# Gated linear attention's result: 16 TensorE transposes replaced by VectorE block transposes and SBUF transfers

## The reference, cut to what matters

```
o_gla = gated_linear_attention(...)                      # [256 tokens, 4 heads x 256]
o_gla = rms_norm_2(o_gla, gla_out_norm_g).reshape(b, s, 1024) * silu(p_r)
gates = sigmoid(p_gate + branch_gate_bias).reshape(b, s, 2, 1024)
mixed = gates[:, :, 0] * (o_attn @ w_attn_branch) + gates[:, :, 1] * (o_gla @ w_gla_branch)
x = x + mixed @ w_out
```

## Time and profile before

| | |
|---|---|
| median of 3 runs | 791.87 us |
| span of the profiled execution, first to last instruction | 790.3 us |
| median of the runs above that span | 1.57 us |
| PE busy | 785.6 us (99%), 4684 matmuls |
| DVE busy | 594.2 us (75%) |
| ACT busy | 469.6 us (59%) |
| DMA traffic | 143.49 MB, mean 182 GB/s |

### The profile page before, as it was taken

One profiled execution on the slowest core, in us unless ns is written; L12 is line 12 of the kernel. 1 busy time (PEld: TensorE's weight loads), 2 busy tenths in 40 slices (PEclk: granted clock), 3 DMA queues, 4 the chain that ended last, 5 costly groups with the idle time before them and its releaser, 6 DMA issues.

```text
span 790.3 us, 12177 instructions
## 1 busy us (share of the span) xinstructions
PE 785.6 (99%) x4684; PEld 667.0 (84%) x4684; DVE 594.2 (75%) x977; ACT 469.6 (59%) x673; POOL 4.5 (1%) x16
## 2 busy tenths in 40 slices
PE   9999999999999999999999999999999999999998
PEld 7888889888888888888888888888888888888886
DVE  6996789987878788679898973677775765556654
ACT  6876556655656666987566655656644654434542
POOL 0000000000000000000000000010000000000000
PEclk9999999999999999999999999999999999999999
DMA  9873354664655663736645376323656555665551
GB/s 325 285 256 107 108 160 160 214 208 164 203 187 194 200 229 113 248 125 212 211 140 182 107 243 230 107 82 134 216 174 194 171 189 177 211 201 177 181 185 53
DMA packets 84653, 143.49 MB, mean 182 GB/s; under 512 B 3904, under 2 KB 44672, under 8 KB 84352
## 3 DMA queue, kind: packets, MB, share of 16 engines
q1 hardware_dynamic: 83888, 141.82, 54.4%
q10 hardware_dynamic: 720, 1.05, 0.4%
HBM read 141.29 MB, written 1.05 MB: 180 GB/s over the span
## 4 chain that ended last, share of the span: by engine, by line
PE 98%; DMA 1%; ACTq 0%; ACT 0%; DVE 0%; issue 0%
PE bank L539 21%; PE bank L540 21%; PE bank L541 21%; PE bank L628 15%; PE bank L633 8%; PE bank L401 3%; PE bank L1039 2%; PE bank L1041 1%; PE bank L612 1%; PE bank L1106 1%; PE bank L1179 1%; DMA arena<-in_x_turned 1%; PE bank L1208 1%; PE bank L615 0%; PE bank L786 0%; PE bank L1136 0%
## 5 line engine op out<-in xcount | busy, mean ns | idle before, releaser
L1901 DVE TENSOR_TENSOR w_lo<-raw,w_hi 128x1024 fp32r<-128x1024 f32 (+1 forms) x254 | 302.5, 1215 | 55.0 <-ACT w_hi L1350 54.2
L1350 ACT CAST w_hi<-raw 128x1024 fp32r<-128x1024 f32 (+1 forms) x254 | 259.8, 1047 | 122.9 <-PE bank L541 112.9
L539 PE MATMUL bank<-w_hi,h_both 128*128 128x512 f32 x352 | 140.4, 399 | 0.0
L540 PE MATMUL bank<-w_lo,h_both 128*128 128x512 f32 x352 | 137.5, 391 | 0.0
L541 PE MATMUL bank<-w_hi,h_both 128*128 128x512 f32 x352 | 137.4, 390 | 0.0
L539 PE MATMUL bank<-w_hi,a_both 128*128 128x512 f32 (+1 forms) x318 | 124.6, 392 | 0.0
L540 PE MATMUL bank<-w_lo,a_both 128*128 128x512 f32 (+1 forms) x318 | 123.6, 389 | 0.0
L541 PE MATMUL bank<-w_hi,a_both 128*128 128x512 f32 (+1 forms) x318 | 123.6, 389 | 0.0
L628 PE MATMUL bank<-a_both,w_hi 128*128 128x512 f32 x512 | 121.5, 390 | 0.0
L628 PEld LDWEIGHTS bank<-a_both,w_hi 128*128 128x128 f32 x512 | 95.5, 188 | 19.3
L539 PEld LDWEIGHTS bank<-w_hi,h_both 128*128 128x128 f32 x352 | 66.2, 188 | 14.4 <-issue 1.5
(11 more groups left out here) (242 smaller groups left out, 891.6 us busy)
## 6 DMA issues: line engine op xcount, KB each, us to landing
raw<-in_w_in SPq DMA_DIRECT2D x45, 1024.0 KB, 5.2
raw<-in_w_up SPq DMA_DIRECT2D x22, 1024.0 KB, 5.1
raw<-in_w_ff_up SPq DMA_DIRECT2D x16, 1024.0 KB, 5.4
raw<-in_w_ff_down SPq DMA_DIRECT2D x16, 1024.0 KB, 5.0
raw<-in_w_down SPq DMA_DIRECT2D x11, 1024.0 KB, 4.9
raw<-in_w_out SPq DMA_DIRECT2D x8, 1024.0 KB, 5.1
raw<-in_w_gla_branch SPq DMA_DIRECT2D x4, 1024.0 KB, 5.1
raw<-in_w_attn_branch SPq DMA_DIRECT2D x2, 1024.0 KB, 5.1
```

The lines of the kernel that those rows point to most:

```text
L539: nc.tensor.matmul(dst, l_hi, r_hi, start=start, stop=False)
L540: nc.tensor.matmul(dst, l_hi, r_lo, start=False, stop=False)
L1350: nc.scalar.copy(dst, raw_half(m % RAW, half, size, cols)).then_inc(s.hi_done, 1)
L1901: nc.vector.tensor_tensor(dst, raw_half(n // 2 % RAW, n % 2, size, cols), h, ALU.subtract).then_inc(s.lo_done, 1)
```

## The change

GLA's result is no longer turned by PE. For each token tile a, DVE turns every 32 x 32 block of the 128 x 1024 tile in place of its partition group (`turn_go`, one instruction into `go_blocks`). SP then issues 16 transfers from SBUF to SBUF (`move_go`), each of 32 partitions x 256 numbers (1 KB of each partition, 32 KB in all), which carry block row i, block column j to block row j, block column i. ACT multiplies the tile by the gain and puts the blocks in order (two instructions of 128 x 512, each waited for), then rounds (one of 128 x 1024) (`go_hi`). DVE makes the low part (`go_lo`). `go_scaled` runs two loop steps earlier in part, so that a tile is complete when its turn comes. Two pairs of semaphores are merged or dropped.

```
-            for m in range(M_GATE + 1, M_FF2):
+            def move_go(a, moves):
+                for n in moves:
+                    i, j = n // 4, n % 4
+                    sp.dma_start(goT[32 * j:32 * j + 32, a, i], go_blocks[32 * i:32 * i + 32, a, j]).then_inc((s.go_in0, s.go_in1)[a], 16)
+            for m in range(M_GATE + 1, M_GATE + 8):
+                load(m)
+            sp.wait_ge(s.go_blocked, 1)
+            move_go(0, range(6))
+            load(M_GATE + 8)
+            move_go(0, range(6, 12))
+            load(M_GATE + 9)
+            move_go(0, range(12, 16))
+            sp.wait_ge(s.go_blocked, 2)
+            move_go(1, range(16))
+            for m in range(M_GATE + 10, M_FF2):
                 load(m)
...
-            pe.wait_ge(s.gla_ready, 1)
-            pe.wait_ge(s.att_masked, 2 * AH)
-            pe.wait_ge(s.gate_free, 6)
-            turn_tiles(4, lambda a, k: go[:, a, k * P:(k + 1) * P], s.go_turned, (0, 1))
-            fill(2)
-            pe.wait_ge(s.att_pt, AH)
-            turn_tiles(4, lambda a, k: go[:, a, 512 + k * P:640 + k * P], s.go_turned, (4, 5))
+            fill(4)
             att_value(AH - 2)
             att_value(AH - 1)
-            fill(4)
+            fill(2)
+            pe.wait_ge(s.att_masked, 2 * AH)
...
-            pe.wait_ge(s.go_lo, 4)
+            pe.wait_ge(s.go_lo, 2)
...
+            def go_hi(a):
+                act.wait_ge((s.go_in0, s.go_in1)[a], 256)
+                for half in range(2):
+                    tiles = goT[:, a].rearrange("p i (k h t) -> p h k i t", h=2, t=32)[:, half]
+                    dst = go_gained[:, a].rearrange("p (k h) (i t) -> p h k i t", h=2, i=4)[:, half]
+                    link(nc.scalar.activation(dst, tiles, ACT.Copy, scale=column("gla_out_norm_g_2", half)))
+                nc.scalar.copy(h2_hi[:, :, a * P:(a + 1) * P], go_gained[:, a]).then_inc(s.go_hi, 1)
...
-            turned_hi(a_hi, 4, 4, s.go_turned, 0, lambda k: column("gla_out_norm_g_2", k % 2), s.go_hi, (0, 1))
-            turned_hi(a_hi, 8, 4, s.go_turned, 2, lambda k: column("gla_out_norm_g_2", k % 2), s.go_hi)
+                if v == AH - 1:
+                    go_hi(0)
+            go_hi(1)
...
+            def turn_go(a):
+                dve.wait_ge(s.gla_ready, a + 1)
+                nc.vector.transpose(go_blocks[:, a].rearrange("p j (k t) -> p k j t", t=32),
+                                    go[:, a].rearrange("p (k j c) -> p k j c", j=4, c=32)).then_inc(s.go_blocked, 1)
+            def go_lo(a):
+                dve.wait_ge(s.go_hi, a + 1)
+                ts = slice(a * P, (a + 1) * P)
+                nc.vector.tensor_tensor(h2_lo[:, :, ts], go_gained[:, a], h2_hi[:, :, ts].bitcast(F32), ALU.subtract).then_inc(
+                    s.go_lo, 1)
...
-            turned_lo(a_lo, a_hi, 4, 4, s.go_hi, 0, lambda k: column("gla_out_norm_g_2", k % 2), s.go_lo, (0, 1))
-            turned_lo(a_lo, a_hi, 8, 4, s.go_hi, 2, lambda k: column("gla_out_norm_g_2", k % 2), s.go_lo)
+            go_lo(0)
+            go_lo(1)
             gate_scaled(3)
```

More of the change, by code:

```diff
@@ L196 @@
 SEMAPHORES = (
-    "x_in first_x0 first_x1 first_x2 first_x3 first_x4 first_w0 first_w1 first_w2 first_w3 first_w4 first_w5 first_w6 first_x_top first_x_lo first_x_hi first_w_hi first_w_lo slab2_half act_warm pe_warm ident_in pos_in consts_in decay_in vecs_in fw_in gate_up_in levels_in dil_in v_far_in out_stored "
+    "x_in first_x0 first_x1 first_x2 first_x3 first_x4 first_w0 first_w1 first_w2 first_w3 first_w4 first_w5 first_w6 first_x_top first_x_lo first_x_hi first_w_hi first_w_lo slab2_half warmed ident_in pos_in consts_in decay_in vecs_in fw_in gate_up_in levels_in dil_in v_far_in out_stored "
     "hi_done lo_done mm_done acc_free0 acc_free1 "
@@ L216 @@
     "gla_e gla_qe gla_level gla_taken gla_o gla_go gla_ssq gla_ready gate_free gate_done "
-    "go_turned go_hi go_lo "
+    "go_blocked go_in0 go_in1 go_hi go_lo "
     "att_squared att_ms root_guessed root_found att_scaled att_turned att_T "
     "att_scores att_masked att_exp att_normed att_turnedp att_pt att_pv oa_hi oa_lo "
-    "bias_in gate_half mix_scaled mix_taken mix_ready mix_turned mix_hi mix_lo "
+    "bias_in gate_half mix_scaled mix_ready mix_turned mix_hi mix_lo "
     "up_low up_summed up_square up_hi up_lo last_down"
@@ L370, in two_blocks_kernel @@
         go_squares = area(7168, GH * GV)
+        go_blocks = area(0, TT, 4, 8 * 32)
+        goT = area(5120, TT, 4, 8 * 32)
+        go_gained = area(0, TT, 8, P)
         gates = (area(3072, TT, D), area(7168, TT, D))
@@ L663, in h_ready @@
                 return lambda k: pe.wait_ge(s.h_lo_done, 4 * norm + k // 2 + 1) if k % 2 == 0 else None
-            pe.wait_ge(s.pe_warm, 1)
+            pe.wait_ge(s.warmed, 1)
             for _ in range(4):
@@ L1394, in _ @@
                 load_x(q)
-            act.wait_ge(s.act_warm, 1)
+            act.wait_ge(s.warmed, 2)
             nc.scalar.copy(st[:, 95:96], st[:, 94:95])
@@ L1953, in rotate @@
                 return nc.vector.tensor_tensor(x2, x2, t1, ALU.add)
-            nc.vector.memset(warm, 0.0).then_inc(s.pe_warm, 1)
-            nc.vector.memset(st[:, 94:95], 0.0).then_inc(s.act_warm, 1)
+            nc.vector.memset(warm, 0.0).then_inc(s.warmed, 1)
+            nc.vector.memset(st[:, 94:95], 0.0).then_inc(s.warmed, 1)
             for k in range(KT):
@@ L2497, in go_scaled @@
                                                          silu_r[:, r, cols], ALU.mult, ALU.mult)
-                if pair_ == GH - 1:
+                if pair_ % 2 == 1:
                     ins.then_inc(s.gla_ready, 1)
+            def turn_go(a):
[7 more added lines that the diff above has]
+                    s.go_lo, 1)
             dve.wait_ge(s.dil_in, 16)
@@ L2520, in _ @@
                         dve.wait_ge(acc_free[c % 2], c // 2 + 1)
-                if 3 <= v < 7:
-                    go_scaled(v - 3)
+                if v == 3:
+                    go_scaled(0)
+                    go_scaled(1)
+                elif v == 4:
+                    turn_go(0)
+                    go_scaled(2)
+                elif v == 5:
+                    go_scaled(3)
                 if v == 5:
@@ L2528, in _ @@
                     out_lo(0)
+                if v == 5:
+                    turn_go(1)
                 if v == 0:
@@ L2581, in _ @@
             dve.wait_ge(s.acc_free1, 14)
-            mixed(1, slice(0, 1)).then_inc(s.mix_taken, 1)
+            mixed(1, slice(0, 1))
             dve.wait_ge(s.mm_done, n + 12)
```

## The result

The changed kernel takes 799.92 us (median of 5 runs, 798.96 to 800.42) against 792.03 us of the kernel before in 5 runs: a ratio of 1.0096, 95% interval 1.0086 to 1.0107. It is slower by 7.9 us. Slower was forecast, by 1.9 us to 793.8 us, and 799.92 lies outside the range of 791.3 to 796.9 us.

A forecast was written before the change was run, and what follows sets the result against it. PE's queue was taken to bound the kernel: PE saves 1.8 us of transposes, then waits 3.7 us for `go_lo`, so the span of 790.3 us becomes 792.2; with 1.57 us outside it, 793.8 us. Range 791.3 to 796.9 us.

The forecast's parts named there:

- PE's saving: On PE, GLA's 16 transposes fall away ahead of GLA's product: 1.78 us.
- The transpose: DVE's turning of one 128 x 1024 tile: 1.2 us, upper bound 2.2 us.
- its covers: On DVE, idle time and waits hide the earlier `go_scaled` and tile 0's transpose; PE's `lo` has 1.6 us to spare.
- SP's load: Load of M_BR + 1 on SP, ahead of 20 moves, issued at 538.5 us after DVE's `lo`.
- Landing of the last move: Tile 1's last move lands 2.0 us after its issue at 548.8 us, at 550.8 us.
- What lies outside the span: Measured time of a run above the profile's span: 1.57 us, as in the kernel before.
- The rival of slow forms: DVE transposes of 2.2 us each give 795.8 us, scattered instructions on ACT 795.0 us; chance 0.12.
- the cheap issue: SP's moves follow each other in less than 0.39 us, so ACT sets the end: 791.3 us; chance 0.22.
- the whole gain: The chain to `go_lo` is done by 550.73 us, PE saves its 1.8 us: 790.1 us; chance 0.03.
- One sum: Upper end of the forecast's case, SP's moves at 0.45 to 0.58 us: 792.5 to 795.2 us; chance 0.53.
- I take 0.52 us: SP's step from one move's issue to the next, bounds 0.41 and 0.57 us; last move issued at 548.8 us.
- The second term that was missing: Clock falls in PE's wait; first half of GLA's product at half speed loses 2.7 us more: 796.5 us; chance 0.10.

The follow-up runs named there:

- e3: Changed kernel with tile 1's moves carrying 8 numbers of each partition instead of 256, all moves still issued: 799.33 us.
- e8: Kernel before with 28 unused transfers behind SP's last load, in four groups of seven, from HBM or SBUF, 32 or 128 partitions: 791.84 us.
- e2: Changed kernel with 27 unneeded matmuls on PE ahead of its wait for the turned result: 797.46 us.
- e4: Changed kernel with all remaining moves of tile 0 and those of tile 1 ahead of the second load of the GLA weights: 795.93 us.
- e6: Changed kernel with moves ahead of that load, five of tile 1 issued by ACT, and a shorter, reordered chain on ACT and DVE: 790.24 us.
- e7: As e4, with 13 unneeded matmuls on PE ahead of its wait: 794.04 us.
- e1: Changed kernel with only one of tile 1's 16 moves issued, part of the result left out: 792.21 us.
- e5: Changed kernel with eight of tile 1's 16 moves issued by POOL instead of SP: 792.48 us.

## Why the prediction was wrong

The way of the argument held, step by step. PE's saving: 1.75 us, forecast 1.78. The transpose: 1.24 us, forecast 1.2; its covers held (`go_scaled` runs one loop step earlier for three of its four parts, nowhere two), and SP's load went at 538.51, forecast 538.5. Landing of the last move: issued at 551.85, ACT began at 553.71, 1.9 us, forecast 2.0. `go_hi`: 2.55 us, forecast 2.3, since each of the two scaling instructions took 0.73 us instead of the 0.62 of the earlier trace rows. `go_lo`: 1.23, forecast 1.2. What lies outside the span: 2.1 us in the profiled run, forecast 1.57. The rival of slow forms, the cheap issue and the whole gain are refuted by these rows and by the step of 0.63 us. One sum was off: at a step of 0.58 us it gives 794.9 us, not 795.2.

The step that failed is "I take 0.52 us" for SP's issues, with 0.57 us as the upper bound. It was 0.63 us, and one of the 20 took 1.56 us; the last move was issued at 551.85 instead of 548.8, 3.05 us late. Of these about 2.1 us are the step and 1.0 us the one long issue, for which the sum had no term. The earlier trace rows held the right number: of the two transfers from SBUF the first took 0.53 us and the second 0.59. I used the distance between their starts, which contains the first one's duration. In a series it is the later one's duration, 0.59, plus the gap of 0.04 that repeats. And I averaged it with four transfers from HBM, on the ground that they are small; e3 and e8 show that smallness does nothing and the source does. Why one issue of a series is longer (1.56, 1.49 and 1.39 us in the change, e3 and e2) stays open; e4, e6 and e7 have such issues of 1.0 to 1.4 us too, e1, e5 and the 28 of e8 have none. The Trainium skill's page "DMA: Bandwidth & Descriptors", section "Issuing engines are not separate DMA queues", says that the time to initiate a DMA is usually small relative to the DMA itself. That does not hold here: an issue takes 0.59 us against a landing of 1.8 us, 20 of them take 13.5 us, and e5, with a second issuing engine, won back 7.4 us.

The second term that was missing, 2.8 us, stood in the prediction as a rival: 2.7 us, with a chance of 0.10. The error was to hold it beside the forecast, although the forecast itself had PE stand still for 3.7 us: e4's wait of 3.4 us had it too, and it cost 1.6 us there. That the size came out so near is partly luck: it assumed that the slow stretch ends with the first half of the product, for which no row spoke, and the three waits in which the clock fell cost 2.8, 2.0 and 1.6 us. With SP's step alone put right the sum gives 795.9 us, inside the range, with the long issue 796.9 us, and with the clock 799.7 us.

## What to carry to other kernels

When work is taken from the engine that bounds the kernel and cut into many small transfers, count the issues, multiply by the repeating step of that queue for that kind of source, and start the sum at the event that lets the queue go on. If the sum ends after the bounding engine arrives, spread the issues over idle queues or put them ahead of loads that have time; here that, with a shorter chain on ACT and DVE, turned 7.9 us of loss into 1.6 us of gain (e6). And price a wait of TensorE with the slow matmuls that may follow it: 1.6 to 2.8 us in these traces, nothing behind waits of 1.3 us.

## What the runs showed of the hardware that was not expected

In a series, an issue on SP holds it 0.59 to 0.60 us when the source is SBUF and 0.42 to 0.43 us when it is HBM, whether 32 or 128 partitions (e8) and, from SBUF, 1 or 32 KB (e3). On POOL an issue from SBUF took 0.50 us in the median of eight, and these ran beside SP's (e5); on ACT five took 0.61 to 0.64 us (e6). In the waits of PE of 6.7, 6.5 and 3.4 us (the change, e3, e4) the granted clock fell to 0.50, and the matmuls behind lost 2.8, 2.0 and 1.6 us; in those of 1.2 and 1.3 us (e1, e5) it stayed at 1.00. A VectorE transpose of 32 x 32 blocks over 128 x 1024 fp32 numbers took 1.24 us, as long as a subtraction of that size.
